# Even mixer: attention begun behind the blocks' products, the compressed branch and the gate inside its steps, and keys doubled by GpSimd

## What is computed

```python
a_in, q, kc, vc, ksl, vsl, kw, vw, gl = split_cols(h @ w_in, EVEN_SPLITS)
a_out = chunked_gmlp(a_in, sgu_norm, sgu_w, sgu_b)           # gate: u * (w @ norm(v) + b)
b_out = nsa_attention(partial_rope(q_raw, cos, sin), q_raw,
                      compress_blocks(kv(kc), ...), compress_blocks(kv(vc), ...),
                      partial_rope(kv(ksl), cos, sin), kv(vsl),
                      partial_rope(kv(kw), cos, sin), kv(vw),
                      jax.nn.sigmoid(gl).reshape(bsz, seq, B_HEADS, N_BRANCH))
return jnp.concatenate([a_out, b_out], axis=-1) @ w_out
...
blk = t[:, idx] + pos_emb[:, None, :]                         # compress_blocks: 15 blocks of 32 tokens
return jax.nn.gelu(blk @ w1) @ w2
...
o = g[..., 0:1] * o_c + g[..., 1:2] * o_s + g[..., 2:3] * o_w # compressed, selected, window
```

## Time and profile before

| | us |
|---|---|
| median of 3 runs | 1910.74 (1909.17 to 1912.89) |
| the profiled execution | 1912.48 |
| its span, first to last instruction | 1910.7 |
| TensorE busy | 1755.4 (92%) |
| VectorE busy | 1306.7 (68%) |
| ScalarE busy | 898.2 (47%) |
| mean granted clock of TensorE | 0.946 |
| even mixer behind its input product, 269.2 to 382.8 | 113.6 |

### The profile page before, as it was taken

One profiled execution on the slowest core, in us unless ns is written; L12 is line 12 of the kernel. 1 busy time (PEld: TensorE's weight loads), 2 busy tenths in 40 slices (PEclk: granted clock), 3 DMA queues, 4 the chain that ended last, 5 costly groups with the idle time before them and its releaser, 6 DMA issues.

```text
span 1910.7 us, 29054 instructions
## 1 busy us (share of the span) xinstructions
PE 1755.4 (92%) x11846; PEld 1565.1 (82%) x11846; DVE 1306.7 (68%) x2315; ACT 898.2 (47%) x1648; POOL 8.4 (0%) x18
## 2 busy tenths in 40 slices
PE   5999987989999999997999997996798779999997
PEld 5999865789999999986899997994697766666664
DVE  6666742677887888766678786657674666666664
ACT  5444631564445444452544444443321446666662
POOL 0000000000000000000000000000000000000000
PEclk9999997999999999997799998998898889999998
DMA  7645522046655566640246662440100528888871
GB/s 304 237 180 192 227 77 78 1 155 264 239 217 207 204 237 247 242 190 6 116 164 230 256 239 99 177 155 1 45 1 23 203 95 340 339 342 341 341 287 67
DMA packets 48517, 351.79 MB, mean 184 GB/s; under 512 B 5504, under 2 KB 5632, under 8 KB 6144
## 3 DMA queue, kind: packets, MB, share of 16 engines
q1 hardware_dynamic: 47952, 348.07, 47.9%
q10 hardware_dynamic: 432, 1.87, 0.2%
HBM read 348.87 MB, written 1.05 MB: 183 GB/s over the span
## 4 chain that ended last, share of the span: by engine, by line
PE 82%; DVE 12%; ACT 3%; issue 1%; DMA 1%; DVEq 0%; ACTq 0%; SPq 0%
PE ps L391 21%; PE ps L393 20%; PE ps L392 20%; PE ps L2396 6%; DVE WL L385 2%; PE ps L1007 1%; PE ps L1741 1%; PE ps L1721 1%; PE ps L868 1%; PE ps L1747 1%; PE ps L1631 1%; PE ps L1163 1%; DVE acc L702 1%; DMA ring<-in_w 1%; PE ps L941 1%
## 5 line engine op out<-in xcount | busy, mean ns | idle before, releaser
L391 PE MATMUL ps<-HH,WH 128*128 128x256 f32 x1696 | 489.3, 289 | 37.0 <-DVE WL L385 23.7
L385 DVE TENSOR_TENSOR WL<-ring,WH 128x512 fp32r<-128x512 f32 x728 | 448.5, 685 | 53.6 <-ACT WH L377 49.5
L393 PE MATMUL ps<-HH,WL 128*128 128x256 f32 x1696 | 484.3, 286 | 0.0
L392 PE MATMUL ps<-HL,WH 128*128 128x256 f32 x1696 | 484.0, 285 | 0.0
L377 ACT ACTIVATE WH<-ring 128x512 fp32r<-128x512 f32 x728 | 391.5, 618 | 96.6 <-PE ps L393 81.7
L391 PEld LDWEIGHTS ps<-HH,WH 128*128 128x128 f32 x1696 | 325.7, 192 | 39.8 <-DVE WL L385 18.2
L392 PEld LDWEIGHTS ps<-HL,WH 128*128 128x128 f32 x1696 | 325.5, 192 | 0.1
L393 PEld LDWEIGHTS ps<-HH,WL 128*128 128x128 f32 x1696 | 325.2, 192 | 0.0
L2348 DVE TENSOR_TENSOR EL<-ring,EH 128x1024 fp32r<-128x1024 f32 x140 | 164.8, 1220 | 76.7 <-ACT EH L2341 76.7
L391 PE MATMUL ps<-AH,WH 128*128 128x256 f32 x704 | 200.7, 285 | 6.8 <-DVE AL L671 6.8
L392 PE MATMUL ps<-AL,WH 128*128 128x256 f32 x704 | 200.2, 284 | 0.0
(11 more groups left out here) (475 smaller groups left out, 2596.6 us busy)
## 6 DMA issues: line engine op xcount, KB each, us to landing
ring<-in_w SPq DMA_DIRECT2D x292, 1024.0 KB, 5.0
AR<-in_w SPq DMA_DIRECT2D x35, 1024.0 KB, 4.8
cols<-in_s SPq DMA_DIRECT2D x1, 2994.0 KB, 12.9
cons<-in_k ACTq DMA_DIRECT2D x1, 1698.0 KB, 13.8
XT<-in_x SPq DMA_DIRECT2D x1, 1024.0 KB, 5.4
out<-SQ SPq DMA_DIRECT2D x4, 256.0 KB, 2.3
cols<-in_s ACTq DMA_DIRECT2D x1, 126.0 KB, 5.6
pos<-in_p ACTq DMA_DIRECT2D x1, 1.0 KB, 7.7
```

The source lines that it names most:

```text
L385: ins = v.tensor_tensor(lo(n)[:, s], ring[:, i % RING, s], hi(n)[:, s].bitcast(F32), ALU.subtract)
L391: pe.matmul(out, ah, bh, start=start, stop=False, skip_group_check=skip)
L392: pe.matmul(out, ah, bl, start=False, stop=False, skip_group_check=skip)
L393: return pe.matmul(out, al, bh, start=False, stop=stop, skip_group_check=skip)
```

## The change

- The rotation comes first on VectorE, right behind the copy of the raw queries. The six `kct` copies, the additions into `blk` and the copies of groups 3, 5 and 7 follow.
- The six `kct` transposes go to six banks, 2 to 7, without waits between them. ScalarE's copy of each piece now waits for VectorE's.
- TensorE transposes the rotated queries and keys ahead of the blocks' products. The rotated keys are doubled by GpSimd in `kv2`, once TensorE has read the former contents, and 12 full transposes take the place of the 24 half-height instructions.
- The attention begins behind the blocks' products. Everything of steps 4 and 6 (hidden transposes, `KCB`, `VB`, gate, compressed scores, softmax, transposes, output) becomes steps that run one by one at the end of each iteration: `pe_even_side`, `act_even_side`, `dve_even_side`. On VectorE the step stands ahead of finishing item i-1.
- All six short items come first, then the six long ones. The outputs of all items go to bank 6 alone (`out_bank`), so outputs of item i wait for `finish` of item i-1. The side steps use bank 7, and bank 5 while items are short; the first long turn waits for `v_cm` for that.
- The compressed output goes to `Ob` by an addition through `ctmp`, and branch 0 of the attention writes `Ob` without adding.
- `VB` is copied by 4 instructions instead of 12.

```diff
@@ pe_turn, pe_outs, dve_outs
+                if c and not i0:
+                    q.wait_ge(v_cm, 2)
...
+        def out_bank(i, i0):
+            return 6 + i % 2 if i0 else 6
...
-            ob = 6 + i % 2
+            ob = out_bank(i, i0)
...
-            if i >= 2:
-                q.wait_ge(v_o, i0 + i - 1)
+            if i >= 2 or (i and not i0):
+                q.wait_ge(v_o, i0 + i - 1 if i0 else i)
@@ pe_attention, and act_attention likewise
+                next(side, None)
@@ even_items
-                      for br in range(2) for th in range(2) for g in range(3)]
+                      for th in range(2) for br in range(2) for g in range(3)]
@@ new: pe_even_side, one step for each iteration of the attention
+            for w in range(2):
+                q.wait_ge(a_hid, 2)
+                for c in range(2):
+                    m = pe.transpose(ps[:, (7, 5)[w], 45 * c:45 * c + 45], hidt[0:45, w, c * 128:(c + 1) * 128], ident[0:45, 0:45])
+                m.then_inc(*q.up(p_hid))
+            yield
+            q.wait_ge(v_ev, 6)
...
+            m.then_inc(*q.up(p_kc))
+            yield
+            q.wait_ge(v_ev, 8)
...
+            m.then_inc(*q.up(p_vb))
+            for a in range(2):
+                q.wait_ge(v_ev, (7, 9)[a])
+                for g in range(4):
+                    m = pe.matmul(ps[:, (7, 5)[a], g * 64:(g + 1) * 64], sw[:, g, :], vS[:, a, g * 64:(g + 1) * 64], start=True, stop=True)
+                m.then_inc(*q.up(p_sg))
+                yield
+            for a in range(2):
+                q.wait_ge(v_sg, a + 1)
+                for p in range(6):
+                    m = pe.matmul(ps[:, (7, 5)[a], p * 30:(p + 1) * 30], QN[:, 6 * a + p, :], KCB[:, p // 2].rearrange("p b n -> p (b n)"), start=True, stop=True)
+                m.then_inc(*q.up(p_cs))
+                yield
+            yield
+            for a in range(2):
+                q.wait_ge(v_cp, 2)
+                if a:
+                    q.wait_ge(v_co, 2)
+                for g in range(3):
+                    m = pe.transpose(ps[:, 7, g * 128:(g + 1) * 128], pc[:, a, 4 * g:4 * g + 4, :].rearrange("p h n -> p (h n)"), ident)
+                m.then_inc(*q.up(p_ct))
+                yield
+                q.wait_ge(a_ct, a + 1)
+                for gs in ((0, 1), (2,)):
+                    if gs == (2,):
+                        q.wait_ge(v_co, 2 * a + 1)
...
+                    yield
@@ new: dve_even_side, from its middle
+            before(0)
+            yield
+            behind(0)
+            before(1)
+            yield
+            behind(1)
+            yield
+            yield
@@ pe_even
+            q.wait_ge(v_ev, 1)
+            copied(q, 1)
+            copied(q, 2)
+            pe_heads(pe, q, pairs(eZ, 512, 6), 3, [0, 1])
+            q.wait_ge(a_kt, 2)
+            q.wait_ge(v_kt, 2)
+            q.wait_ge(g_kv, 8)
+            pe_heads(pe, q, [kv2[:, th, h // 3, h % 3].rearrange("p c d -> p (c d)") for h in range(6) for th in range(2)], 6, [2, 3])
             q.wait_ge(d_mats, 16)
-            q.wait_ge(v_ev, 1)
+            q.wait_ge(v_ev, 2)
...
-            pe_heads(pe, q, twice(eZ, 1280, 6), 6, [2, 3])
@@ act_even, the kct copies
+                    q.wait_ge(v_kt, i + 1)
@@ dve_even
             copy_heads(v, q, QN, 12, 0, [0, 1], 1)
+            q.wait_ge(p_hT, 3)
+            dve_rope(v, q, eZ, 512, 18, 64, 8, eTmp, v_ev)
...
+            copy_heads(v, q, eQT, 12, 3, [0, 1], 1)
+            copy_heads(v, q, eKT, 12, 6, [2, 3], 1)
...
+            def every_other():
+                while True:
+                    next(steps, None)
+                    yield
+                    yield
+            q.wait_ge(a_gate, 1)
+            dve_attention(v, q, even_items, 0, 0, ePT, finish, every_other())
@@ pool_even
+            q.wait_ge(p_kt, 6)
+            q.wait_ge(v_ev, 1)
+            for a in range(2):
+                for w in range(2):
+                    src = eZ[:, a, 1280 + 192 * w:1280 + 192 * (w + 1)].rearrange("p (h d) -> p h d", h=3)
                     pool.tensor_copy(kv2[:, a, w], src.unsqueeze(2).broadcast_to([P, 3, 2, 64])).then_inc(*q.up(g_kv))
```

More of the change, by code:

```diff
@@ L1014, in dve_outs, with pe_attention @@
             q.wait_ge(p_o, i0 + i + 1)
-            finish(v, q, items[i], ps[:, 6 + i % 2, 0:256].rearrange("p (h d) -> p h d", h=4), stats[:, i, 8:12])
-        def pe_attention(pe, q, items, i0, s0, PT, first):
+            finish(v, q, items[i], ps[:, out_bank(i, i0), 0:256].rearrange("p (h d) -> p h d", h=4), stats[:, i, 8:12])
+        def pe_attention(pe, q, items, i0, s0, PT, first, side=iter(())):
             n = len(items)
@@ L1025, in pe_attention, with act_attention @@
                     pe_outs(pe, q, items, i - 1, i0, s0, PT)
-        def act_attention(act, q, items, i0, ch0, PT):
+                next(side, None)
+        def act_attention(act, q, items, i0, ch0, PT, side=iter(())):
             n = len(items)
@@ L1166, in pe_even @@
                         m.then_inc(*q.up(p_raw))
[L1167 to L1173, removed]
-                for c in range(2):
-                    m = pe.matmul(ps[r0:r0 + 64, 4, 0:45], C("w2k", 64 * c, 64 * c + 64), hid[:, 0, c, :], start=c == 0, stop=c == 1)
@@ L1213, in first @@
             def first(q):
-                for g in range(4, 9):
+                for g in range(3, 9):
                     copied(q, g)
-                q.wait_ge(v_co, 2)
-            pe_attention(pe, q, even_items, 0, 0, ePT, first)
+            pe_attention(pe, q, even_items, 0, 0, ePT, first, pe_even_side(pe, q))
         def act_even(act, q):
@@ L1337, in finish @@
                 q.own()
-                v.tensor_tensor(otmp, o, r.unsqueeze(2).broadcast_to([P, 4, 64]), ALU.mult).then_inc(*q.up(v_o))
-                q.own()
                 z = Ob[:, th, heads[0]:heads[0] + 4, :]
-                v.tensor_tensor(z, z, otmp, ALU.add).then_inc(*q.up(v_fin))
-            dve_attention(v, q, even_items, 0, 0, ePT, finish)
+                if br == 0:
+                    v.tensor_tensor(z, o, r.unsqueeze(2).broadcast_to([P, 4, 64]), ALU.mult).then_inc(*q.up(v_o))
+                else:
+                    v.tensor_tensor(otmp, o, r.unsqueeze(2).broadcast_to([P, 4, 64]), ALU.mult).then_inc(*q.up(v_o))
+                    q.own()
+                    v.tensor_tensor(z, z, otmp, ALU.add).then_inc(*q.up(v_fin))
+            steps = dve_even_side(v, q)
+            def every_other():
+                while True:
+                    next(steps, None)
+                    yield
+                    yield
+            q.wait_ge(a_gate, 1)
+            dve_attention(v, q, even_items, 0, 0, ePT, finish, every_other())
         def pool_even(pool, q):
```

204 lines of the change are left out of this document (94 added, 110 removed).

## The result

| | before | changed |
|---|---|---|
| median, runs beside each other | 1911.82 (4 runs, 1909.17 to 1913.06) | 1889.62 (4 runs, 1887.47 to 1894.18) |
| the profiled execution | 1912.48 | 1887.47 |
| its span | 1910.7 | 1885.7 |
| even mixer, first transpose to output product | 113.6 | 90.67 |

The changed kernel ran eleven more times beside experiments: medians 1886.98 and 1886.91, lowest 1881.66, highest 1896.41 (ratios 0.9876 and 0.9871).

The account below looks back on a forecast made before the run. TensorE was taken to bound the kernel (82% of the chain), with 39.85 us between products and attention half idle or at low clock. +5.4 - 1.1 - 39.85 + 12.65 = -22.9 us gave 1888, range 1880 to 1908.

Parts of the forecast that it names:

- Part 1: Ahead of the blocks' products: rotation first, 12 full key transposes for 24 half-height instructions; products start at 283.6, 5.4 us later.
- rival D: GpSimd's doubled keys come late, needing over 5 us beyond 1.85; 1891 at 3 us beyond that; no separate chance given.
- Part 2: Blocks' products: clock rises sooner behind the transposes, so 15.0 us, 1.1 less; bounds 13.9 and 16.1.
- Part 3: Stretch between the products' end and the attention's start: 39.85 us leave the front.
- Part 4: Even attention with the side steps in it: 61.3 us against 48.65, 12.65 more.
- t=57.8, the plan before its additions: Attention's end counted at full clock, before adding 1.0 us for some ten waits and 2.5 for a clock drop.
- Rival B: Clock falls at the attention's start, short steps cost 6.4 to 7.2 us: +14, 1902; chance 0.23.
- a clock of 1.00 over the first 20 us: Sign at the attention's start: full clock there shows the prediction right, a fall there shows it wrong.
- the main case: Whole kernel: the summed forecast holds, 1888, between 1881 and 1894; chance 0.63.
- A: The prediction's main case for the whole kernel: 1888, between 1881 and 1894; chance 0.63.
- Rival C: Low clock in the long attention steps too, 8.0 us each against 4.2; up to 1925; chance 0.14.
- The prediction's remark under B: Attention: long scores would raise a fallen clock, since they stood ahead of the rise at 347.2 before.

Follow-up runs that it names:

- keys_alone: Kernel before, with only GpSimd's doubling of the rotated keys and 12 full transposes for 24 half-height instructions: 1897.94, ratio 0.9943.
- keys_by_tensor: Changed kernel with the keys' doubling undone, TensorE again writing both halves in 24 half-height instructions: 1909.40, ratio 0.9985.
- filled_ten: Changed kernel with 10 useless 128 x 256 products in TensorE's 5.07 us wait ahead of transpose group 5: 1886.95, ratio 0.9879.
- side_steps_first: Changed kernel with all side steps (compressed branch and gate) run as a block ahead of the attention: 1905.67, ratio 0.9975.
- changed_again: The changed kernel itself, unedited, run again beside experiments: 1886.98 (5 runs).
- changed_third: The changed kernel itself, unedited, run once more beside experiments on one chip: 1886.91 (6 runs).
- copy_ahead: Changed kernel with VectorE's copy of transpose group 3 put ahead of the twelve additions into blk: 1886.94, ratio 0.9885.
- filled_copies: Changed kernel with 21 useless 128 x 256 products in TensorE's 5.07 us wait ahead of transpose group 5: 1891.71, ratio 0.9899.
- both_short_edits: Changed kernel with copy_ahead's and first_half_alone's edits together: 1883.69, ratio 0.9876.
- both_and_filled: both_short_edits plus useless products: 4 ahead of transpose group 5, 2 and 1 at the attention's start: 1879.55, ratio 0.9838.
- filled_start: Changed kernel with 5 and 3 useless 128 x 256 products in TensorE's first two waits of the even attention: 1887.37, ratio 0.9870.
- first_half_alone: Changed kernel where the transposes of the first half's `pc` wait for that half alone, not both: 1888.06, ratio 0.9889.

## Why the prediction was right

Times below count from the mixer's start or, with t, from the first score product.

- **Part 1, products 14.4 us after the start.** Measured 14.50. VectorE's row was as laid out: rotation to 4.6, copies, additions to 10.0, the copy of group 3 (0.69), a wait of 5.07 for TensorE where 5 was foreseen, 16 transposes in 3.70 at a clock of 0.50 (3.45 predicted). GpSimd's copies began at 4.71 and took 1.86, so rival D had no ground. keys_alone and keys_by_tensor give the keys 9.7 and 8.2 us in their profiles, in both directions, against 11.6 less 2.6 worked out. The medians give 12.1 and some 20, the latter mostly at lower clock.
- **Part 2, products 15.0.** Measured 14.72 here, 14.60 and 13.94 in the other two profiles of the same kernel, so full-clock 13.9 was right as a bound. Behind the transposes the clock rose 1.6 us into the products, where 2.3 were foreseen. In keys_alone transposes at a clock of 0.50 stand ahead of the rise at 307.4 as well, with 1.5 us of gate products between. In filled_ten 16 such transposes ran at 1.00. The Trainium skill (TensorE: Matmul & The Clock Gate, section Part 4: PE-mode transpose) says the full clock does not engage for transposes. This case's traces do not agree: with the transposes ahead of them the products took 13.94 to 14.98 us in every run, and 16.3, near the former 16.1, only in keys_alone, where they are not ahead.
- **Part 3, 39.85 off the front.** The stretch is gone. side_steps_first shows that moving this work ahead of the attention instead of into it gives up most of the gain: all of it in its profiled mixer, 18 of 22 us in the medians.
- **Part 4, attention 61.3.** Measured 61.45, in part by errors that cancel. First turn t=3.7 (3.73), second 6.5 (6.95), outputs, `VB` and gate done at 10.2 (10.8), short steps done at 20.8 (21.6), `pc` transposes at 30.7 (31.25) after a wait of 2.7 (2.58). From there to output 11 24.05 us were foreseen and 26.27 measured. `VB`'s four copies, taken as 0.34, were 0.354. Against t=57.8, the plan before its additions, the `pc` transposes came 0.55 us later, output 11 another 2.22 and the end another 0.88: 3.65 in all, where I had added 2.5 for one fall of the clock at the wait and 1.0 for ten small waits. The term that was mis-sized is the clock. There were three low stretches, 3.4 us long at the start, 3.4 behind the wait and 2.9 in the tail, at means of 0.95 and 0.90 over the halves: 0.05 of 31.25 and 0.10 of 30.2 are 4.6 us, an upper bound, since part of it fell on waits. Beyond the waits that the plan had, the trace shows only a few tenths. That the sum came out within 0.15 us is in part luck: the same kernel's attention took 62.33 us in changed_again and 66.52 in changed_third.
- **Rival B, the clock falls at the start, +14.** I gave it 0.23 and wrote that a clock of 1.00 over the first 20 us would show the prediction right and a fall there would show it wrong. By this sign the main case was wrong: the fall came in all three profiles of the changed kernel, for 3.4, 3.4 and 17.1 us. It left the medians in the main range because it was short or was paid back in part. B's price was right for the full length: in filled_ten, low for 30.7 us, the transposes of `pc` ended at t=44.8 (45 predicted), and the attention was 12.7 us longer than the changed kernel's. changed_third's 17.1 us cost 4.1 in the mixer, since the low behind the `pc` wait did not come that time. So A and B are not two cases but the ends of one spread, and it is part of why executions run from 1882 to 1896. The range from 1880 to 1908 held all fifteen.
- **Rival C, low clock in the long steps.** It did not come: behind the `pc` wait the clock was low for 3.4 us in the changed kernel and 6.8 in changed_again, about one long step, and then again only in the tail. The prediction's remark under B, that the long scores would raise the clock, fits the two longest stretches but is not shown. In side_steps_first the clock was low over all six short items and rose at 353.9, behind the first scores of 256 keys at 350.07. In filled_ten it rose at 333.7, behind those at 329.62:

```profile
325.37 1.81 PE L1021 MATMUL ps<-AR 128*128 128x64 f32 x8
326.97 2.71 PE L1189 MATMUL ps<-AR 128*128 128x30 f32 x12
329.62 2.08 PE L949 MATMUL ps<-AR 64*128 64x256 f32 x8
...
334.31 1.14 PE L949 MATMUL ps<-AR 64*128 64x256 f32 x8
```

  One score group of 64x256 takes 2.08 us ahead of the rise and 1.14 behind it. In copy_ahead, changed_third and filled_copies (low for 23.9 us) the clock rose earlier, among the short steps, so long scores are not needed for it.

## What to carry to other kernels

Work that fills another stage's waits is worth its own length and, beyond that, the clock: the same side steps done apart cost 22.6 us more in the profiled executions here, some 7 of them an attention at lower clock. Where such a stage starts thin, look at several profiles of the same kernel before pricing the clock; one profile shows one length of the low stretch. And when a wait is removed, read which engine's instruction stands next in line (here ScalarE's copy behind a Gelu) before expecting more than the first step.

## What the runs showed of the hardware

- The same instruction stream got low stretches of 3.4 to 17.1 us at the attention's start in three profiles; in filled_ten it was 30.7 us, with TensorE busy throughout. The small products of the short steps stood in all of them. What ends such a stretch early or late is open.
- The eight falls at the attention's start come in two groups. In four (changed, changed_again, both_short_edits, keys_by_tensor) the products ahead had begun at 0.50, the fall came 3.8 to 4.0 us after the first scores and lasted 3.4 us, 13.7 in keys_by_tensor. In the others (changed_third, copy_ahead, filled_copies, filled_ten) the products had run at 1.00 from end to end in 13.94 or 13.95 us, the fall came 6.0 to 6.5 us after the first scores and lasted 17.1 to 30.7. So products at full clock went with a longer low stretch behind them, except in both_and_filled, where the start was filled too. The cause is not shown.
- In both kernels with extra products in the thin start (filled_start, both_and_filled) the clock stayed at 1.00 there (for 31.5 us from the first scores in filled_start, 56.7 in both_and_filled); without them it fell in eight of the nine profiles of this attention, all but first_half_alone's. That the gaps cause the fall is likely, not proven: two profiles stand for it.
- A product of 128 x 256 in f32 is two records and 0.43 us at full clock (5 of them in 2.16 us in filled_start, 301.19 to 303.35); my expectations had taken one record for one product.
